# A mixer and attention model with two expert layers: experts in 25 blocks, outputs scattered to token order, five weight buffers

## The reference, cut to what matters

```python
g_sel = argmax(p_g); top_v, top_i = top_k(sel, 2)              # 1 of 4 groups, 2 of its 8 experts
gate = w_g[:, None] * softmax(top_v)                           # one weight per token and expert
y = (silu(x @ w_gate[e]) * (x @ w_up[e])) @ w_down[e]          # 1024 -> 256 -> 1024
out[token] += y * gate                                         # two experts for each token
```

## Time and profile before

| what | value |
|---|---|
| median of 3 runs | 2150.88 us (2149.66 to 2151.88) |
| span of the profiled execution, first to last instruction | 2143.7 us |
| PE busy, DVE busy, ACT busy, POOL busy | 2004.4, 812.5, 532.2, 188.4 us |
| mean granted TensorE clock | 0.964 |
| DMA: queue of SP and queue of POOL | 289.63 MB and 43.13 MB |

### The profile page before, as it was taken

One profiled execution on the slowest core, in us unless ns is written; L12 is line 12 of the kernel. 1 busy time (PEld: TensorE's weight loads), 2 busy tenths in 40 slices (PEclk: granted clock), 3 DMA queues, 4 the chain that ended last, 5 costly groups with the idle time before them and its releaser, 6 DMA issues. The chain is left out here.

```text
span 2143.7 us, 28374 instructions
## 1 busy us (share of the span) xinstructions
PE 2004.4 (94%) x11085; PEld 1161.1 (54%) x11085; DVE 812.5 (38%) x1889; ACT 532.2 (25%) x1294; POOL 188.4 (9%) x283
## 2 busy tenths in 40 slices
PE   8999999889997988999998999999999988999990
PEld 4545554488543964444445657777675554444440
DVE  1114555867353463111115524444352134111115
ACT  1003233433111321111133433333331110111112
POOL 0000002001162211000002000000000001000003
PEclk9999999989998989999999999999999988999995
DMA  3500100020021147999985000000020018999987
GB/s 138 226 28 6 40 20 4 1 82 4 2 90 53 41 175 302 403 423 426 424 335 204 23 0 1 1 1 1 1 80 23 30 46 331 387 425 424 425 354 265
DMA packets 51389, 334.68 MB, mean 156 GB/s; under 512 B 6832, under 2 KB 7152, under 8 KB 33200
## 3 DMA queue, kind: packets, MB, share of 16 engines
q1 hardware_dynamic: 39376, 289.63, 33.1%
q0 software_dynamic: 11872, 43.13, 5.5%
HBM read 285.48 MB, written 47.25 MB: 155 GB/s over the span
## 5 line engine op out<-in xcount | busy, mean ns | idle before, releaser
L221 PE MATMUL psum<-arena 128*128 128x512 f32 (+12 forms) x9694 | 1863.2, 385 | 79.6 <-issue 29.0
L221 PEld LDWEIGHTS psum<-arena 128*128 128x128 f32 (+3 forms) x9694 | 1010.5, 168 | 877.7 <-issue 783.6
L2193 DVE TENSOR_TENSOR arena<-psum,arena 128x256 f32<-128x256 f32 x50 | 21.2, 425 | 423.1 <-ACT arena L2243 423.1
L1541 ACT ACTIVATE arena<-arena 128x1024 f32<-128x1024 f32 x43 | 45.4, 1056 | 249.7 <-DVE arena L2940 105.6
L2279 POOL DMA_INDIRECT arena<-xn_rows,arena x50 | 47.2, 944 | 657.4 <-PE psum L2154 443.4
L2243 ACT ACTIVATE arena<-psum 128x256 f32<-128x256 f32 x50 | 19.2, 385 | 322.0 <-PE psum L221 322.0
L2853 ACT ACTIVATE arena<-psum,arena 128x1024 f32<-128x1024 f32 (+8 forms) x72 | 50.2, 699 | 188.6 <-DVE arena L2889 188.6
L1242 ACT ACTIVATE arena<-psum 128x256 f32<-128x256 f32 (+3 forms) x128 | 44.0, 356 | 102.3 <-PE psum L221 91.4
L2236 ACT ACTIVATE arena<-psum 128x512 f32<-128x512 f32 x50 | 29.9, 597 | 148.1 <-PE psum L221 148.1
L2882 DVE TENSOR_TENSOR psum<-psum,arena 128x128 f32<-128x128 f32 (+2 forms) x72 | 20.3, 283 | 103.5 <-PE psum L221 103.2
L2387 DVE SCALAR_TENSOR_TENSOR arena<-arena 128x1024 f32<-128x1024 f32 (+1 forms) x34 | 43.5, 1281 | 30.7 <-DMA arena<-expert_rows,arena 29.4
(11 more groups left out here) (303 smaller groups left out, 1306.5 us busy)
## 6 DMA issues: line engine op xcount, KB each, us to landing
arena<-in_w_exp SPq DMA_DIRECT2D x64, 2048.0 KB, 18.4
arena<-in_w_exp SPq DMA_DIRECT2D x64, 1024.0 KB, 17.7
expert_rows<-arena SPq DMA_DIRECT2D x66, 512.0 KB, 14.9
arena<-in_x SPq DMA_DIRECT2D x16, 512.0 KB, 4.6
xn_rows<-arena SPq DMA_DIRECT2D x16, 512.0 KB, 2.6
arena<-in_w_out SPq DMA_DIRECT2D x8, 512.0 KB, 8.1
arena<-in_w_o SPq DMA_DIRECT2D x1, 4096.0 KB, 12.3
out<-arena SPq DMA_DIRECT2D x8, 512.0 KB, 5.3
```

Source lines behind the costliest of these rows:

```text
L221: return e.matmul(out, lhsT, rhs, start=start, stop=stop, skip_group_check=True)
L1541: return e.activation(junk, h[:, s, :], ACT.Square, accum_out=sq_sum[:, s:s + 1])
```

## The change

The 25 blocks stay, in a slightly other order, and a planner gives each expert one of five buffers (`BUFFER`) and the block after which it is loaded (`AFTER`). Four experts instead of three are put ahead. The five first loads are issued one after the other; the fifth, rank 18, waits for the third round of the sort, and the wait for gathers is gone. The table carries `2 * token + choice` instead of the token, and the gate beside it, so the one-hot matmul has 82 columns instead of 41. An empty slot gets an index out of range, which the gather and the new scatter leave out. The capacity and the base of a rank come from a small matmul (`caps`), during which a second sort round runs. VectorE and ScalarE multiply with the gate when they evict, and POOL scatters the rows to `expert_rows` in the order token, choice. The combine is then one plain transfer of 1 MB per token tile, issued by SP, and two plain adds. The zero fill and its waits are gone, the three latent weights are issued by POOL, and the router's transposed tiles use two buffers in turn. Cut to its core:

```diff
-N_BIG = 18
-N_PAIRS = (NE - N_BIG) // 2
...
+N_FIRST, LEAD = 4, 1 << 16
...
+NM = 25
 NBLK = NM + NOV
-PAIR_AT = (3, 6, 9, 12, 16, 19, 22)
...
-N_FIRST, LEAD = 3, 1 << 16
...
+N_BUF = 5
...
+SEQ = [0, 1, 2, 3, 18, 4, 19, 5, 6, 20, 7, 8, 21, 9, 10, 11, 22, 12, 13, 23, 14, 15, 24, 16, 17]
...
+BUFFER, AFTER, _free = [], [], [(-1, _i) for _i in range(N_BUF)]
+for _n in range(NE):
+    _free.sort()
+    _at, _buf = _free.pop(0)
+    assert _at < USED[_n][0]
+    AFTER.append(_at)
+    BUFFER.append(_buf)
+    _free.append((USED[_n][-1], _buf))
+FREED, TOP_BUFFER = min(_free)
...
-        m_fill = [d_fill.nth() for _ in range(NM, NBLK)][-1]
...
-            e.wait_ge(*m_zero)
-            for b in range(NM, NBLK):
-                e.dma_start(y_dram[P * b:P * (b + 1), :], zero_rows).then_inc(d_fill.sem, 16)
...
-            e.tensor_tensor(y.tokf, y.tokf, y.valid, ALU.mult).then_inc(*V.up())
-            e.tensor_scalar(y.full, y.io32, float(P), float(P), ALU.mult, ALU.add).then_inc(*V.up())
+            for j in range(2):
+                e.tensor_scalar(y.code[j], y.tokf, 2.0, float(j - EMPTY), ALU.mult, ALU.add).then_inc(*V.up())
+            e.wait_ge(*V.last())
+            for j in range(2):
+                e.tensor_tensor(y.code[j], y.code[j], y.valid, ALU.mult).then_inc(*V.up())
...
+            e.tensor_tensor(y.above, bc_mid(y.key, NE), bc_last(y.key, NE), ALU.is_gt).then_inc(*V.up())
+            after()
+            e.tensor_reduce(y.place, y.above, AX.X, ALU.add).then_inc(*V.up())
+            after()
+            for j, what in enumerate(("rank_cap", "rank_base")):
+                e.tensor_scalar(y.by_rank[0:NE, j, :], y.place[0:NE], col("rank_no", 0, NE), col(what, 0, NE), ALU.is_equal,
+                                ALU.mult).then_inc(*y.placed.up())
...
+            next_eight(1)
+            e.wait_ge(*y.tb.full("caps"))
+            cap, base = (y.tb.bank["caps"][:, NE * j:NE * (j + 1)] for j in range(2))
+            e.tensor_tensor(y.cnt, y.cnt, cap, ALU.subtract).then_inc(*V.up())
+            e.tensor_tensor(over, rank, bc_mid(cap, ns), ALU.is_ge).then_inc(*V.up())
...
+                e.tensor_tensor(y.eq[j], bc_mid(y.io48, ns), blks[:, :, j:j + 1].to_broadcast([P, ns, NBLK]), ALU.is_equal).then_inc(*V.up())
+            after()
+            for j in range(2):
+                e.tensor_tensor(y.blk1[j][:, :, 0:NBLK], y.eq[j], bc_last(y.code[j], NBLK), ALU.mult).then_inc(*V.up())
+                e.tensor_tensor(y.blk1[j][:, :, NBLK:], y.eq[j], y.gates[:, :, j:j + 1].to_broadcast([P, ns, NBLK]), ALU.mult).then_inc(*V.up())
...
-            e.tensor_copy(idx.bitcast(I32), y.tb.bank["idx"][:, 0:NBLK]).then_inc(*y.tb.drain("idx", "V"))
+            e.tensor_scalar(to_row.bitcast(I32), y.tb.bank["idx"][:, 0:NBLK], float(EMPTY), None, ALU.add).then_inc(*y.indexed.up())
+            e.wait_ge(*y.indexed.last())
+            e.tensor_scalar(from_row.bitcast(I32), to_row.bitcast(I32), 1, None, ALU.logical_shift_right).then_inc(*y.indexed.up())
+            e.tensor_copy(gate_of, y.tb.bank["idx"][:, NBLK:2 * NBLK]).then_inc(*y.tb.drain("idx", "V"))
...
-            keep_busy(e, banks[7], 11)
+            keep_busy(e, banks[7], 3)
+            e.wait_ge(*y.placed.at(2))
+            mm(e, y.tb.bank["caps"][:, 0:2 * NE], ones[0:NE, :], y.by_rank[0:NE].rearrange("p a b -> p (a b)"), True,
+               True).then_inc(*y.tb.fill("caps"))
+            keep_busy(e, banks[7], 8)
...
         def sp_gate_up(e, y, n):
-            if n >= 4:
-                e.wait_ge(*y.ex.full(("gu", LOADED[n - 4][1])))
-            e.dma_start(y.gu[n % 4], weights_of(e, y, n)[:, 0:WG]).then_inc(d_gu[n % 4].sem, 16)
+            if AFTER[n] >= 0:
+                e.wait_ge(*y.ex.full(("gu", AFTER[n])))
+            e.dma_start(y.gu[n], weights_of(e, y, n)[:, 0:WG]).then_inc(d_gu[BUFFER[n]].sem, 16)
         def sp_down(e, y, n):
-            if n >= 4:
-                e.wait_ge(*y.ex.full(("y", LOADED[n - 4][1], 1)))
-            e.dma_start(y.dn[n % 4], weights_of(e, y, n)[:, WG:]).then_inc(d_dn[n % 4].sem, 16)
+            if AFTER[n] >= 0:
+                e.wait_ge(*y.ex.full(("y", AFTER[n], 1)))
+            e.dma_start(y.dn[n], weights_of(e, y, n)[:, WG:]).then_inc(d_dn[BUFFER[n]].sem, 16)
...
-                e.activation(y.y[b % 3][:, half_cols(1)], y.ex.bank[key], ACT.Copy, bias=0.0).then_inc(*y.ex.drain(key, "S"))
+                e.activation(y.y[b % 3][:, half_cols(1)], y.ex.bank[key], ACT.Copy, bias=0.0,
+                             scale=gate_of[:, SEQ[b]:SEQ[b] + 1]).then_inc(*y.ex.drain(key, "S"))
...
-                e.tensor_copy(y.y[b % 3][:, half_cols(0)], y.ex.bank[key]).then_inc(*y.ex.drain(key, "V"))
+                e.tensor_scalar(y.y[b % 3][:, half_cols(0)], y.ex.bank[key], gate_of[:, SEQ[b]:SEQ[b] + 1], None,
+                                ALU.mult).then_inc(*y.ex.drain(key, "V"))
...
         def gather(e, xe, block, sem):
             e.indirect_dma_start(out=xe, out_offset=None, in_=xn_dram[:, :],
-                                 in_offset=bass.IndirectOffsetOnAxis(idx.bitcast(I32)[:, block:block + 1], 0)).then_inc(sem, 16)
+                                 in_offset=bass.IndirectOffsetOnAxis(from_row.bitcast(I32)[:, block:block + 1], 0),
+                                 bounds_check=L - 1, oob_is_err=False).then_inc(sem, 16)
+        def scatter(e, rows, block, sem):
+            e.indirect_dma_start(out=y_dram[:, :], out_offset=bass.IndirectOffsetOnAxis(to_row.bitcast(I32)[:, block:block + 1], 0),
+                                 in_=rows, in_offset=None, bounds_check=2 * L - 1, oob_is_err=False).then_inc(sem, 16)
         def pool_experts(e, y):
-            e.wait_ge(*y.tb.empty("idx"))
+            e.wait_ge(*y.indexed.at(2))
             for p in range(y.ns - 3, y.ns):
                 e.wait_ge(*y.m_xs[p])
-            for b in range(NM):
-                if b >= 3:
-                    e.wait_ge(*y.ex.full(("x", b - 3, 1)))
-                gather(e, y.xe[b % 3], SEQ[b], d_xe[b % 3].sem)
-        def sp_store(e, y, b):
-            e.wait_ge(*y.ex.empty(("y", b, 0)))
-            e.wait_ge(*y.ex.empty(("y", b, 1)))
-            e.dma_start(y_dram[P * SEQ[b]:P * (SEQ[b] + 1), :], y.y[b % 3]).then_inc(d_y[b % 3].sem, 16)
+            for b in range(3):
+                gather(e, y.xe[b], SEQ[b], d_xe[b].sem)
+            for b in range(NM + 2):
+                if b + 3 < NM:
+                    e.wait_ge(*y.ex.full(("x", b, 1)))
+                    gather(e, y.xe[b % 3], SEQ[b + 3], d_xe[b % 3].sem)
+                if b >= 2:
+                    for hf in range(2):
+                        e.wait_ge(*y.ex.empty(("y", b - 2, hf)))
+                    scatter(e, y.y[(b - 2) % 3], SEQ[b - 2], d_y[(b - 2) % 3].sem)
...
+            n = over_count(e)
+            wait_all(e, y.m_y[-3:])
...
         def dve_combine(e, y, s, c, m_c):
             n = SLOT[s][1]
+            e.wait_ge(*m_c)
             for j in range(2):
-                e.wait_ge(*m_c[j])
                 if j:
                     e.wait_ge(*y.h_out.last())
-                e.scalar_tensor_tensor(out=h[0:n, s, :], in0=c[j][0:n, :], scalar=gates[0:n, s, j:j + 1], in1=h[0:n, s, :], op0=ALU.mult,
-                                       op1=ALU.add).then_inc(*y.h_out.up())
-        def pool_combine(e, s, c, sems):
+                e.tensor_tensor(h[0:n, s, :], h[0:n, s, :], c[0:n, j, :], ALU.add).then_inc(*y.h_out.up())
+        def sp_combine(e, s, c, sem):
             n = SLOT[s][1]
-            for j in range(2):
-                e.indirect_dma_start(out=c[j][0:n, :], out_offset=None, in_=y_dram[:, :],
-                                     in_offset=bass.IndirectOffsetOnAxis(dest.bitcast(I32)[0:n, s, j:j + 1], 0)).then_inc(sems[j].sem, 16)
+            e.dma_start(c[0:n].rearrange("p a b -> p (a b)"), y_pairs[P * s:P * s + n, :]).then_inc(sem.sem, 16)
...
+        def sp_latent(e):
+            for s in range(NS):
+                if s >= 2:
+                    e.wait_ge(*layers[0].h_out.at(2 * (s - 2) + 2))
+                sp_combine(e, s, c_lat[s % 2], d_c[s % 2])
...
-            for n in range(3):
+            for n in range(N_BUF):
                 sp_gate_up(e, y, n)
                 sp_down(e, y, n)
-            for b in range(2):
-                e.wait_ge(*y.m_xe[b])
-            sp_gate_up(e, y, 3)
-            sp_down(e, y, 3)
             for b in range(NM):
-                for n in y.of[b]:
-                    if n + 4 < NE:
-                        sp_gate_up(e, y, n + 4)
-                if b:
-                    sp_store(e, y, b - 1)
-                    for n in y.of[b - 1]:
-                        if n + 4 < NE:
-                            sp_down(e, y, n + 4)
+                for n in range(NE):
+                    if AFTER[n] == b:
+                        sp_gate_up(e, y, n)
+                for n in range(NE):
+                    if b and AFTER[n] == b - 1:
```

(23 more changed lines are left out.)

## The result

| | before | after |
|---|---|---|
| median of 5 runs each | 2150.88 us (2142.10 to 2152.72) | 2161.33 us (2158.61 to 2164.25) |
| span of the profiled execution | 2143.7 us | 2159.4 us |
| mean granted TensorE clock | 0.964 | 0.960 |

The two spans differ by 15.7 us, the medians by 10.5: each run after lasted about 1.9 us longer than its span (2161.33 against 2159.4 in the profiled one).

A forecast was written before the change was run, and what follows sets the result against it. The prediction took PE to bound the expert loops, with losses in stretches without expert work. Terms 0.4 + 4.1 + 3.5 + 4.4 - 0.7 + 0.9 - 0.6 = +12.0 us gave 2163 us, range 2147 to 2174.

The forecast's parts named there:

- The base: Starting time of the sum: the terms, made against the profiled span of 2143.7 us, were added to the median, 2150.88 us.
- Ids: Four added VectorE operations in the ids, on PE's path before pooling in layer 0, covered in layer 1: +0.4 us.
- the zero fill's 0: Removing the zero fill, its waits and the memset, covered by PE's projection work, was to change nothing: 0 us.
- Table to gather: Table stage up to the first gather's issue: later by 0.9 us in layer 0 and 0.6 us in layer 1.
- Gather against weights: First gather running beside weight loads, landing in 8.5 us instead of 4.5: PE starts experts +4.1 and +3.5 us later.
- Clock: PE idles before the experts, then runs four to five us at half speed: +2.2 us in each layer.
- Loops: Expert loops: the weights' stall of 0.66 us goes, the rest stays under PE: -0.7 us in all.
- Hand-over: From layer 0's experts to the latent stage: VectorE's second add of the first tile ends later, +0.9 us.
- Tail: After the last block: VectorE's adds start at 2107.5 us and end at 2139.5 us, -0.6 us.
- Rival A: First gather slips in between weight packets, landing in 6.5 us, clock kept: +3.6 us, 2154.5 us; chance 0.28.
- B: Rival: faster, through tail, hand-over, loops and a first gather landing in 4.5 us: -4.9 us, 2146 us; chance 0.14.
- C: Rival: POOL's queue chokes on gathers and scatters in the loop, 0.5 us a block: +25, 2188 us; chance 0.08.

The follow-up runs named there:

- run 1: Changed kernel with the fourth and fifth weight loads of each layer held until the first two gathers have landed; 2147.35 us, ratio 0.9998 to the kernel before.
- run 2: Changed kernel with only the fifth weight load of each layer held until the first two gathers have landed; 2147.12 us, ratio 1.0001 to the kernel before.
- run 5: Changed kernel with only the down half (1 MB) of the fifth load held until the first two gathers have landed; 2154.67 us, ratio 1.0040 to the kernel before.
- run 4: Changed kernel with empty slots' index clamped to the last token's row, so each gather fetches 128 rows; 2163.59 us, ratio 1.0074 to the kernel before.
- run 3: Changed kernel with eleven instead of five PE warm-up products after the index matmuls, loads unchanged; 2159.84 us, ratio 1.0049 to the kernel before.
- run 6: run 1 plus 17 instead of 13 warm-up products at the hand-over to the latent stage; 2146.11 us, ratio 0.9989 to the kernel before.
- run 7: run 6 plus index conversion ahead of the last sort rounds and counts, and warm-up products raised from eight to eleven and five to seven; 2138.06 us, ratio 0.9959.
- run 9: run 7 without its added warm-up products, keeping the earlier index conversion on VectorE; 2146.74 us, ratio 0.9987 to the kernel before.
- run 8: run 7 without its change of order on VectorE, keeping the added warm-up products; 2146.30 us, ratio 0.9986 to the kernel before.

## Why the prediction was right, and where it was not

The forecast was the case that came: a first gather that lands beside the weights, an idle PE, a dropped clock; 2163 us against 2161.33. The size agrees better than its parts do, and that is in part luck.

**The base.** The sum was added to the median 2150.88 us of three runs, though its terms came from an execution of about 2145.6 us. Over the 21 to 23 runs of before beside the experiments the median was 2147.5 to 2149.6 us. So the base was 1 to 5 us high, and the sum below too small by about as much: the two errors cancel.

**Ids, +0.4:** VectorE's stretch from L1875 on made PE's wait 10.60 us for the 10.25 in the earlier trace rows, +0.35. Right. The other 1.9 us of the first stretch can't be told from the differences between executions (last section), so the zero fill's 0 isn't tested either.

**Table to gather, +0.9 and +0.6:** measured +1.85 and +2.25; the step was sized at a half and at a quarter of what came. The second index operation was priced at 0.2 us; from the first index operation to the gather pass 1.33 us in layer 0 (814.17 to 815.50), 0.49 before. Each gather now has a register move of POOL's queue ahead of it on its line, which the gather of before hadn't, and 0.9 us lie between the end of the index and the gather's start, 0.3 before. That the move, or the bound that it may serve, costs the 0.6 us wasn't tried. Another 1.2 and 1.1 us are in VectorE's capacity steps: from the ranking's reduction to the first one-hot 12.26 us for 11.05 in layer 0, 11.73 for 10.59 in layer 1, where I had taken new and old steps as even and added 0.65.

**Gather against weights, +4.1 and +3.5** with the terms above in them, so 3.2 and 2.9 of their own: measured +3.8 and +3.95 to PE's start. The place and the size were right, shown by runs 1, 2 and 5. The working was not: I scaled between two rows by the rows fetched, and run 4 shows that the number of rows doesn't matter; what the fifth load has queued does. The scaling wasn't even carried through: 4.5 + 0.6 x 6.5 is 8.4, and layer 1's 53 rows would have given 7.2 us, where 9.5 were measured. Had the routing filled the blocks, the step would have given 11 us, wrongly.

**Clock, +2.2 each:** measured +3.7 and +3.0, outside the stated bounds of 0 and 2.6 (run 3 takes them away again with the landings unchanged). I had costed four to five us at half speed; the window 824 to 832 us is at 0.50 throughout.

**Loops, -0.7 in all:** measured -1.0 in each layer. I found the weights' stall of the earlier trace rows in layer 1 only. The same stall stood in layer 0: there too one pair of blocks starts 12.41 us apart before, and 11.70 after. The other 0.3 us is one interval of 11.7 that became 11.4 with the new order of the pairs.

**Hand-over, +0.9:** +0.5 to the first latent transposes, near enough; then +2.0 up to the third group of latent products, a clock term that was counted in the table stage and left out here. PE timeline of the kernel before:

```profile
1131.01 1.09 PE L2545 MATMUL psum<-arena 128*128 128x128 f32 x8 [3.40 <-DVE arena L2631]
1135.31 11.55 PE L221 MATMUL psum<-arena 128*128 128x384 f32 x32 [3.20 <-issue]
...
1149.66 9.71 PE L221 MATMUL psum<-arena 128*128 128x384 f32 x32 [1.93 <-ACT arena L2566]
```

The clock fell there before, too: the first group took 11.55 us, the second 9.71 again. After the change they took 12.10 and 11.40 us. That the longer idle time ahead of the transposes (3.83 for 3.40 us) made the difference isn't shown: with PE kept busy up to the transposes the two groups took 11.40 and 9.71 us in run 6, 11.40 and 11.40 in runs 7 and 9, and 9.71 and 11.40 in run 8, all with the same code there.

**Tail, -0.6:** measured +1.6 to the first add, exactly the 2107.5 us less 2105.91 of the prediction, and -3.4 in the adds, where I had allowed 0.8 us of gaps and a plain add at 1.23 us; they ran at 1.22 without gaps.

**Rival A** (in turn, +3.6) didn't come: landings of 9.0 and 9.5 us, not 6.5. The Trainium skill's rule beside it (DMA: Bandwidth & Descriptors, "Queues, rings and completion order": an engine serves its queues in turn) agrees with the trace from 819 us on, when both queues move (0.11 beside 0.67 MB up to 821 us); it doesn't tell of the 3.5 us before, in which only the weights moved, and of which 2 us pass between issue and first packet in run 2 as well. **B's** tail and loops came about in part (-1.8 and -2.0), but its condition, a first gather that isn't held up, failed; in run 2, where it holds, the time is that of before, not 5 us less. **C** didn't come: from the third block on, blocks start 11.4 to 11.85 us apart, as before but for the two stalls, and PE waits for no rows there.

## What to carry to other kernels

Before a load is issued early "because a buffer is free", look which small transfer will be queued behind it, and who waits for that: here 3 MB sent some 4 us ahead of a gather of a third of a MB at most (78 and 53 rows of 4 KB) cost some 14 us over the two layers, and one wait on the issuing queue gave it back. A wait on the path costs twice where the clock falls with it; cover it with work, and count that work at the clock at which it will run: in run 8 the cover that ended 2.15 us early paid the drop in full, while the one that ended 1.63 us early paid nothing. When two limits stand close together (VectorE's order and PE's clock in the table stage), removing either alone may show nothing, as in runs 8 and 9; try both before you call a stage tight.

## What the runs showed of the hardware that was not expected

One execution differs from the next by more than most terms of this sum. PE's restart in layer 0's table stage stands between 782.7 us (run 2) and 792.5 us (run 8), though the code ahead of it is the same in all runs from 1 to 9. The windows 400 to 560 us of runs 2 and 8, columns as in group 3:

```profile
400.00:560.00 160.00, 138.64 (x3642) 119.51 (x3642) 104.47 (x270) 52.55 (x142) 15.81 (x28) 0.96 0.08 29
```

```profile
400.00:560.00 160.00, 135.84 (x3560) 119.40 (x3560) 105.52 (x269) 51.10 (x137) 13.20 (x24) 0.90 0.08 29
```

The granted clock is 0.96 in the one and 0.90 in the other, in a stretch full of short waits. But this clock doesn't order the runs: run 7 had 0.93 there and reached the restart at 784.67 us, run 1 had 0.94 and reached it at 789.97. What makes the difference stays open. Single runs of the kernel before lay between 2141 and 2154 us. So a part of one stage is read from the stage's own start, never from the absolute times of two profiles, and a difference of 2 us in the median needs more than the 6 to 12 runs that each kernel had here.
